# Seven half products for the first block's up projection, and both outer taps of the value's convolution on VectorE

## What is computed

```
h = rmsnorm(x, norm_ffn_g[l])
u = centred_depthwise_conv(h @ w_up[l], ffn_conv_w[l])      # 3 taps: t-1, t, t+1
u_gate, u_val = jnp.split(u, 2, axis=-1)                    # 2816 channels each
x = x + ((jax.nn.silu(u_gate) * u_val) @ w_down[l]).astype(x.dtype)
```

## Time and profile before

| | us |
|---|---|
| median of 3 runs | 3478.45 |
| lowest, highest | 3478.35, 3479.25 |
| the profiled execution | 3477.65 |
| its span, first to last instruction | 3475.8 |
| busy: TensorE matmul | 3420.4 (98%) |
| busy: GpSimd | 1882.2 (54%) |
| busy: VectorE | 1737.2 (50%) |
| busy: ScalarE | 1222.3 (35%) |
| mean granted TensorE clock | 0.995 |
| chain that ended last: TensorE, VectorE, ScalarE | 91%, 5%, 2% |

### The profile page before, as it was taken

How to read it: one execution, slowest core, us unless ns; L and a number is a source line. 1 busy time by engine, 2 the same in 40 slices (tenths; PEclk the granted TensorE clock), 3 DMA queues, 4 the chain that set the end, 5 groups by cost and what they waited for, 6 DMA issues and landing times.

```text
span 3475.8 us, 51472 instructions
## 1 busy us (share of the span) xinstructions
PE 3420.4 (98%) x19709; PEld 2814.0 (81%) x19709; DVE 1737.2 (50%) x2946; ACT 1222.3 (35%) x2206; POOL 1882.2 (54%) x1148
## 2 busy tenths in 40 slices
PE   8999999999999999999999999999999999999999
PEld 6777778888877768888887787789898888779898
DVE  6466655425546575561541264357374124447463
ACT  4336532201233464220121143236262125236251
POOL 6532355655644333665665544537676556536665
PEclk9999999999999999999999999999999999999999
DMA  3221122322223102232332211213233223213332
GB/s 137 79 82 34 38 87 95 104 84 96 87 84 114 52 2 98 91 106 82 100 100 90 97 62 55 79 61 106 96 104 108 84 90 99 85 55 104 103 104 91
DMA packets 84981, 297.53 MB, mean 86 GB/s; under 512 B 9464, under 2 KB 11640, under 8 KB 84400
## 3 DMA queue, kind: packets, MB, share of 16 engines
q1 hardware_dynamic: 83296, 291.16, 25.3%
q0 software_dynamic: 1296, 3.15, 0.3%
q10 hardware_dynamic: 192, 0.47, 0.1%
HBM read 285.88 MB, written 8.86 MB: 85 GB/s over the span
## 4 chain that ended last, share of the span: by engine, by line
PE 91%; DVE 5%; ACT 2%; issue 1%; POOL 0%; DMA 0%; SPq 0%; DVEq 0%; ACTq 0%; POOLq 0%
PE PSUM L421 19%; PE PSUM L420 19%; PE PSUM L419 19%; PE PSUM L2239 4%; PE PSUM L2241 4%; PE PSUM L2240 4%; PE PSUM L1153 2%; PE PSUM L1154 1%; PE PSUM L1155 1%; DVE SLABS L1826 1%; DVE OUTER_PRODUCT L1823 1%; PE PSUM L1193 1%; PE PSUM L1165 1%; PE PSUM L1177 1%; PE PSUM L2739 1%
## 5 line engine op out<-in xcount | busy, mean ns | idle before, releaser
L325 POOL TENSOR_TENSOR W_LOS<-SLABS,W_HIS 128x1024 fp32r<-128x1024 f32 (+3 forms) x370 | 924.8, 2499 | 30.9
L323 POOL TENSOR_SCALAR W_HIS<-SLABS 128x1024 fp32r<-128x1024 f32 (+3 forms) x370 | 408.6, 1104 | 980.6 <-DMA SLABS<-w_k 961.3
L420 PE MATMUL PSUM<-H_LO,W_HIS 128*128 128x512 f32 x1808 | 714.4, 395 | 0.0
L419 PE MATMUL PSUM<-H_HI,W_HIS 128*128 128x512 f32 x1552 | 618.9, 399 | 0.6 <-issue 0.6
L421 PE MATMUL PSUM<-H_HI,W_LOS 128*128 128x512 f32 x1552 | 616.4, 397 | 0.0
L420 PEld LDWEIGHTS PSUM<-H_LO,W_HIS 128*128 128x128 f32 x1808 | 339.9, 188 | 85.8 <-issue 2.9
L615 DVE TENSOR_TENSOR PSUM<-PSUM,FACTORS 128x512 f32<-128x512 f32 x238 | 165.1, 696 | 472.2 <-PE PSUM L421 434.3
L421 PE MATMUL PSUM<-ACT_HI,W_LOS 128*128 128x512 f32 x928 | 368.8, 397 | 0.0
L419 PE MATMUL PSUM<-ACT_HI,W_HIS 128*128 128x512 f32 x928 | 367.4, 396 | 0.5 <-DVE ACT_LO L570 0.5
L420 PE MATMUL PSUM<-ACT_LO,W_HIS 128*128 128x512 f32 x896 | 354.1, 395 | 0.0
L419 PEld LDWEIGHTS PSUM<-H_HI,W_HIS 128*128 128x128 f32 x1552 | 292.3, 188 | 71.3 <-issue 4.1
(11 more groups left out here) (627 smaller groups left out, 6986.3 us busy)
## 6 DMA issues: line engine op xcount, KB each, us to landing
SLABS<-w_k SPq DMA_DIRECT2D x406, 512.0 KB, 3.5
SLABS<-w_k SPq DMA_DIRECT2D x32, 768.0 KB, 4.1
SLABS<-w_k SPq DMA_DIRECT2D x32, 640.0 KB, 3.9
X<-w_k SPq DMA_DIRECT2D x2, 2048.0 KB, 9.2
SLABS<-w_k SPq DMA_DIRECT2D x16, 256.0 KB, 3.0
ARENA<-gate_rows SPq DMA_DIRECT2D x8, 512.0 KB, 5.8
X<-xT SPq DMA_DIRECT2D x4, 512.0 KB, 6.1
gate_rows<-RT SPq DMA_DIRECT2D x8, 256.0 KB, 2.0
```

What stands on the lines that cost most here:

```text
L323: nc.gpsimd.tensor_scalar(hi, raw, 1.0, 0.0, MUL, ADD).then_inc(pool_step, 1)
L325: nc.gpsimd.tensor_tensor(lo, raw, hi.bitcast(F), SUB).then_inc(slab_split[s], 1)
L419: mm(out, w_hi, rhs[0](k), start=k == first, stop=False)
L420: mm(out, w_hi, rhs[1](k), start=False, stop=False)
```

## The change

The first block's feed-forward part runs through the functions of the second block's. They take a stage number g (0 and 1: first block, 2 and 3: second block) instead of a layer, and `both(g)` is true for the first block, where the value has taps too. The direct functions ffn_pe, ffn_act, ffn_dve and ffn_pool are gone. In part 0 two pairs stay direct, ten become sevens; in part 1 all ten are sevens. The terms N2 and T4 of the first block lie in H_LO, which is free there. Semaphores and their counts are shifted to serve all four stages; the second block's instructions and their order stay.

What is new for `both(g)`: per pair VectorE multiplies the value bank by FACTORS (scale_value), ScalarE makes its middle tap into the new buffer VALUE_UP (in SBUF), VectorE adds both outer taps (value_tap), the second back into the PSUM bank, and the product with Silu is cut in two: 511 columns, and the last column, which the second tap does not reach, from VALUE_UP. VectorE's order is changed too (value11 and the two scalings ahead of the sums), and ScalarE's (value tap, KEPT5, then the gate's Identity, then high6).

```diff
+        VALUE_UP = WORK[:, 12 * SEQ:13 * SEQ]
...
+            def value_taps(part, j):
+                block, value = part * FFN_PARTS[0] + block_of(part, j), BANK[pair_banks(j)[1]]
+                act.wait_ge(*sv_at(g, "scaled", post_count(g, "scaled", part, j, 1)))
+                if block:
+                    act.wait_ge(*sv_at(g, "tap2", post_count(g, "tap2", part, j, 0)))
+                nc.scalar.activation(VALUE_UP, value[:], ACT.Identity, scale=tap_of(g, block, 4)).then_inc(sv["biased"], 1)
...
-                    if done:
+                    if done and both(g):
+                        value_taps(part, j - 1)
+                        if j == SEVENS - 1:
+                            keep6(part)
+                        if j < SEVENS:
+                            keep5(part, j)
                         biased(part, j - 1)
-                    if ahead:
-                        high6(part, j + 1)
...
+                        if ahead:
+                            high6(part, j + 1)
...
+            def scale_value(part, j):
+                b = pair_banks(j)[1]
+                if j < 0:
+                    dve.wait_ge(bank_full[b], need(bank_full[b]))
+                else:
+                    dve.wait_ge(*sv_at(g, "value11", seventh(g, part, j) + 1))
+                    dve.wait_ge(*sv_at(g, "value12", seventh(g, part, j) + 1))
+                nc.vector.tensor_tensor(BANK[b][:], BANK[b][:], FACTORS[:], MUL).then_inc(sv["scaled"], 1)
...
+            def value_tap(part, j):
+                block, value = part * FFN_PARTS[0] + block_of(part, j), BANK[pair_banks(j)[1]]
+                dve.wait_ge(*sv_at(g, "biased", post_count(g, "biased", part, j, 1)))
+                nc.vector.scalar_tensor_tensor(VALUE_UP[:, 1:], value[:, 0:SEQ - 1], tap_of(g, block, 3), VALUE_UP[:, 1:], MUL, ADD).then_inc(sv["tap1"], 1)
+                dve.wait_ge(*sv_at(g, "tap1", post_count(g, "tap1", part, j, 2)))
+                nc.vector.scalar_tensor_tensor(value[:, 0:SEQ - 1], value[:, 1:], tap_of(g, block, 5), VALUE_UP[:, 0:SEQ - 1], MUL, ADD).then_inc(sv["tap2"], 1)
...
             def gated(part, j):
                 buf, b = GT[(part * FFN_PARTS[0] + block_of(part, j)) % 2], pair_banks(j)[1]
...
+                if both(g):
+                    nc.vector.tensor_tensor(BANK[b][:, 0:SEQ - 1], buf[:, 0:SEQ - 1], BANK[b][:, 0:SEQ - 1], MUL)
+                    nc.vector.tensor_tensor(BANK[b][:, SEQ - 1:], buf[:, SEQ - 1:], VALUE_UP[:, SEQ - 1:], MUL).then_inc(sv["product"], 1)
+                else:
+                    nc.vector.tensor_tensor(BANK[b][:], buf[:], BANK[b][:], MUL).then_inc(sv["product"], 1)
...
                 for j in range(SEVENS + 1):
                     done, ahead = j - 1 >= first, j + 1 < SEVENS
+                    if both(g):
+                        if j == SEVENS:
+                            last_value12(part)
+                        if j:
+                            value11(part, j - 1)
+                        if done:
+                            scale_value(part, j - 1)
                     if done:
                         scale(part, j - 1)
                     if ahead:
-                        sums_dve(dve, l, part, j + 1)
-                    if j:
-                        value11(part, j - 1)
+                        sums_dve(dve, g, part, j + 1)
...
                     if done:
                         taps(part, j - 1)
+                    if done and both(g):
+                        value_tap(part, j - 1)
...
-                ffn_pe(pe, f"1{l}")
+                conv_ffn_pe(pe, l)
...
-                model_dve(dve, f"ffn_g{l}", tile_of(H_HI), tile_of(H_LO2))
-                ffn_dve(dve, f"1{l}", f"fconv{l}", None, lambda: next_mix(l + 1))
+                model_dve(dve, f"ffn_g{l}", tile_of(H_HI), tile_of(H_LO2), meanwhile=lambda: terms_dve(dve, l, 0),
+                          before_factors=lambda: terms_dve(dve, l, 1))
+                conv_ffn_dve(dve, l, lambda: next_mix(l + 1))
...
-                    if n < 2:
-                        gemm_sp(sp, w_k8, at, 2 * blocks, KB)
-                    else:
-                        conv_ffn_sp(sp, n - 2, part, at)
+                    conv_ffn_sp(sp, n, part, at)
```

More of the change, by code:

```diff
@@ L306, in split_halved, with split_weights, turn @@
                 nc.gpsimd.tensor_tensor(lo, raw, hi.bitcast(F), SUB).then_inc(slab_split[0], 1)
[L308 removed]
+        def split_weights(pool, slabs, width=KB, first=None, halved=False, amid=None):
             need = need_pool
[L312 removed]
+            def turn(count, first=None, halved=False, amid=None):
                 for s in range(count):
@@ L2011, in gates_dve @@
                 need.seen[bank_free[b].name] = taken[f"gates{l}"][b] + 2
[L2014 to L2042, removed]
-                        else:
[L2044 to L2085, removed]
-                            nc.vector.tensor_tensor(UP[s][:], BANK[v][:], FACTORS[:], MUL).then_inc(bank_free[v], 1)
-                            dve.wait_ge(bank_free[v], need(bank_free[v]))
-                        dve.wait_ge(silu_done, need(silu_done))
-                        value = VALUES[s] if both else UP[s]
-                        if both:
-                            dve.wait_ge(bank_free[v], need(bank_free[v]))
-                        nc.vector.tensor_tensor(value[:], GT[s][:], value[:], MUL).then_inc(dve_step, 1)
-                        dve.wait_ge(dve_step, need(dve_step))
-                        hi, lo = blk(ACT_HI, i * 2 + s), blk(ACT_LO, i * 2 + s)
-                        nc.vector.tensor_copy(hi, value[:]).then_inc(dve_step, 1)
-                        dve.wait_ge(dve_step, need(dve_step))
-                        nc.vector.tensor_tensor(lo, value[:], hi.bitcast(F), SUB).then_inc(act_ready, 1)
-                        if not both:
-                            dve.wait_ge(act_ready, need(act_ready))
-                first += blocks
-                if blocks == FFN_PARTS[0] or after is None:
-                    add_to_x_dve(dve)
-                else:
-                    after()
-                for b in (1, 3):
-                    need.skip(bank_free[b], KB // 4)
@@ new lines, in taps @@
+                first, second = ((1, 0, 0), (0, 1, 2)) if both(g) else ((2, 0, 0), (1, 0, 1))
+                late, early, i = first
+                nc.vector.scalar_tensor_tensor(buf[:, late:], gate[:, 0:SEQ - late], tap_of(g, block, i), buf[:, late:], MUL, ADD).then_inc(sv["tap1"], 1)
+                dve.wait_ge(*sv_at(g, "tap1", post_count(g, "tap1", part, j, 1)))
+                late, early, i = second
+                nc.vector.scalar_tensor_tensor(buf[:, late:SEQ - early], gate[:, early:SEQ - late], tap_of(g, block, i), buf[:, late:SEQ - early], MUL, ADD
+                                               ).then_inc(sv["tap2"], 1)
@@ L2566, in sums_early @@
                 if k == 6:
-                    sums_dve(dve, l, 1, 0)
+                    sums_dve(dve, g, 1, 0)
             sevens(0)
-            add_to_x_dve(dve, factor=True, before=sums_early)
+            add_to_x_dve(dve, factor=not both(g), before=sums_early)
             sevens(1)
```

411 lines of the change are left out of this document (223 added, 188 removed).

## The result

The changed kernel takes 3530.65 us (median of 4 runs, 3528.96 to 3532.82) against 3478.4 us for the kernel before in the same session: ratio 1.0152, 95% interval 1.0134 to 1.0169. It is 52.2 us slower; the forecast was 37.0 us slower, 3515.5 us, with a range to 3534. The profiled execution took 3528.96 us, its span is 3527.0. One execution of a kernel further down, the one with the value's taps cut, took 6141.92 us at a granted clock of 0.815, while its other three agree within 1.7 us; it is left out of that kernel's time.

A forecast was written before the change was run, and what follows sets the result against it. TensorE bounded the kernel before; VectorE was to set the changed turn. Stretches of 123.6 and 118.9 us, 242.5 against 224.0, gave +18.5 a layer, +37.0 on the median 3478.45: 3515.5 us, range 3498 to 3534.

The forecast's parts named there:

- The column is held by GpSimd: First block's 128x1 product on VectorE, two SBUF inputs: waits 1.85 us for GpSimd's 1024-wide subtraction, in seven of ten turns.
- VectorE's turn: VectorE's time per pair in the first block's sevens: 12.27 us with the column held, 10.42 without, against 11.2 direct.
- VectorE, not TensorE, at its best: First block's sevens: even with no column wait VectorE sets the turn, 10.42 us against TensorE's 10.0.
- The two ends of a stretch: Part 0: gate22 of pair 0 at 15.4 us; part 1: 10.2; last turns 10.4 and 9.9 or 10.4, then 2.0.
- The sum: First block's up stretches: 123.6 plus 118.9, together 242.5 us against 224.0, so +18.5 a layer and +37.0 in all.
- seven turns of 12.27 (85.9): Term for the held turns in each part of the first block: seven VectorE turns of 12.27 us, 85.9 us together.
- the first rival: First block's one-column product does not wait for GpSimd: every turn 10.42 us, 10.4 less a layer, 3457.6 us; chance 0.15.
- The column does not wait: Rival: the column's output goes to PSUM, or it slips in ahead of GpSimd's subtraction; 3457.6 us, chance 0.15.
- the slip of 0.42 us: Slip that would put the column ahead of GpSimd's subtraction, making GpSimd wait instead; forecast column start 0.42 us inside it.
- its balance point at 0.7 us of wait: Column wait per turn in the first block below which the change was to be a gain: 0.7 us.
- All hidden: Rival: VectorE's added work is hidden, TensorE runs as in the second block, 200.6 for 224.0; 3431.7 us, chance 0.02.
- Tables reload in every turn: Rival: ScalarE loads tables up to twice, 1.28 us each, in each of 36 turns; about 3608 us, chance 0.02.

The follow-up runs named there:

- one tensor operand: Changed kernel with the one-column product made as tensor times per-partition scalar, order unchanged: 3464.38 us, ratio 0.9961 to the kernel before.
- the column first: Changed kernel with the one-column product issued ahead of the wide 511-column product: 3465.51 us, ratio 0.9965 to the kernel before.
- The run with the wait filled: Changed kernel with product m3 of each first-block pair issued twice, just before TensorE's wait for gate22: 3521.74 us, ratio 1.0125 to the kernel before.
- its two realisations: Changed kernel with the one-column product ahead of the wide one (3465.51 us), or made as tensor times scalar behind it (3464.38 us).
- the fastest version: Changed kernel with HIGH57 and LOW57 made before the activation's high and low parts, and the column as tensor times scalar behind the wide product: 3452.18 us.
- the run in halves: Changed kernel with GpSimd's 1024-wide subtraction in the first block cut into two of 512: 3488.49 us, ratio 1.0031 to the kernel before.

## Why the prediction was right, and where it was short

**The column is held by GpSimd.** Right. Forecast a column of 2.01 us (8.68 to 10.69, of which 1.85 is the wait) in seven of ten turns, ending with GpSimd's subtraction; measured 1.98, ending within 0.03 us of it. Three runs bear on the cause alone: the order, the number of tensor operands, the length of GpSimd's instruction. Each moved the turn by what the lock says.

**VectorE's turn.** Laid out from the spacings of the earlier trace rows it was 12.27 us held and 10.42 free. Measured 12.18 held, 10.41 free in the same order (one tensor operand), 10.36 with the column first. The 0.09 is GpSimd's subtraction, which starts 8.21 us into the turn instead of 8.26 and takes 2.35 us instead of 2.40.

**VectorE, not TensorE, at its best.** Right: 9.98 without the value taps, 10.36 with them. The 10.0 for TensorE came from the earlier trace rows.

**The two ends of a stretch.** Forecast 123.6 and 118.9 us; measured 125.2 and 120.5 in layer 0, 126.6 and 122.0 in layer 1. The first gate22 of part 0 came at 14.2 us of it in layer 0, where the first column took 0.16 us, and at 15.5 us in layer 1, where it took 1.02 (forecast 15.4, with 0.9 for that column). The two turns without a subtraction took 10.35 and 10.17 us in the first stretch (forecast 10.4 and 9.9). What follows the last gate22 took 3.3 us in the first and in the fourth stretch, and 2.1 and 2.3 in the others (forecast 2.0). In the first and the fourth the clock had fallen behind the last wait, of 2.59 and 3.30 us:

```profile
683.20:686.10 2.90, 2.65 (x12) 2.68 (x13) 2.17 (x5) 0.74 (x2) 2.82 (x2) 0.50 0.00 0
1789.10:1792.20 3.10, 2.64 (x12) 2.67 (x13) 2.37 (x5) 0.93 (x2) 2.92 (x1) 0.50 0.00 0
```

Behind the last wait of the second stretch, 3.02 us, it had not.

**The sum, the step that failed.** 485.0 us forecast for the four stretches, 494.3 measured. The term that was mis-sized is "seven turns of 12.27 (85.9)", which measured 86.3 to 88.2 us: it counted TensorE's idle time of some 2 us a turn as that and no more. In the trace, 8 of the 28 held turns and one more near the end of layer 1 are 1.0 us longer, 9 us in all; the two slow ends above add 1.2 each, and the held turns that are 0.09 shorter than forecast take 2.5 off. The run with the wait filled shows that the wait is the cause. That its median is also 9 us lower is luck: it loses some of these 9 us again in the turns that the doubled product lengthens. The missing step is that TensorE, made to wait, also ran at half its clock afterwards.

**Outside the stretches** I had put nothing. There, 5.0 us are in the profiled execution (51.3 us longer than before's, less 46.3): 1.2 in the rest of the two stages and 3.8 outside them. The kernels with a free column have it too: the first rival gave 3457.6, its two realisations measured 3465.5 and 3464.4, though the turns were as laid out and the four stretches only 2.0 and 1.1 us longer. Likewise the fastest version's stretches save 17.4 us in layer 0 and 16.1 in layer 1 against direct pairs, 33.5 in all, and the kernel gains 25 (its traced execution 28.3). The traces place a part of it, at falls of the clock outside the stretches. In the changed kernel 2.1 us are lost near 2890 us, where the second block does the same work before and after, and where the granted clock is 0.50 now and was 1.00 in the kernel before (the same work stood at 2841 to 2851 us there):

```profile
2891.60:2898.20 6.60, 5.71 (x19) 4.10 (x20) 1.50 (x5) 4.19 (x11) 4.04 (x4) 0.50 0.13 47
```

In the fastest version 2.5 us are lost behind the two stretches of layer 1, where the clock is 0.50 for 3.2 us each. Such falls lie at different places in different traces, so that they may belong to the execution and not to the kernel; where the rest lies was not settled.

**The rivals.** "The column does not wait" was right as a mechanism and wrong as a forecast here, since the slip of 0.42 us it needed did not come by itself; its balance point at 0.7 us of wait fits the run in halves (0.74 us over the free 0.16, a turn of 11.1, +0.3%). "All hidden" needed VectorE's stalls of 0.56 us out: in that order the turns are TensorE's 9.98, but a layer's two stretches are 206.6 us (207.9 in layer 1) and not its 200.6, and the whole is 3452.2, not 3431.7. "Tables reload in every turn" did not happen: Silu's line (L2288) took 0.62 to 0.64 us in all its instances, and no load stands in a turn.

**The change's purpose** stands apart from its defect. Sevens in the first block are worth 25 us (3452.2), if the column is written so that GpSimd can't hold it and VectorE's order leaves it no stall.

## What to carry to other kernels

An instruction's size says nothing of its cost if it can be locked out: look for VectorE instructions with two tensor inputs in SBUF that stand near GpSimd work and ahead of something TensorE waits for, however small they are, and write them with one tensor operand (a per-partition scalar, or an input in PSUM). Moving such an instruction ahead of the one that locks it out helps where the timing holds and fails at the ends of the loop; changing its operands helped in all 44 places here. And where a change makes TensorE wait in each turn of a loop, count more than the wait: look at the granted clock behind the gaps.

## What the runs showed of the hardware that was not expected

A per-partition scalar read from SBUF does not make a VectorE instruction one with two SBUF inputs: 216 ns in the middle of a GpSimd subtraction, against 1.98 us for the same product as tensor times tensor.

Even a GpSimd instruction with a single tensor operand (L325, 128x1536) held the two-input column, 1.40 us, to its own end. The kernel before had a short case of it already in the earlier trace rows: the product of 0.52 us stood beside L323, which has one tensor operand too.

TensorE's granted clock fell to 0.50 for 3.2 us behind a gap of about 2 us, in some turns and not in others of the same layout, and at the ends of stretches behind single waits of 2.5 to 3.3 us, again in some and not in all; with the wait filled (25.3 us in 34 waits, 0.74 each) no turn was long by the clock, where 67.1 us in 36 (1.86 each) had brought nine. More work for TensorE made the kernel faster, by 9 us.
